# A three-block model on one core: shifts of the first norm on TensorE, its scales before the root, gates beside the query linear

## The reference

```python
cond_lat = silu(c); cond_ctx = silu(c_ctx)
m_lat = split(cond_lat @ mod_w[0] + mod_b[0], 6)      # shift, scale, gate, shift, scale, gate
m_ctx = split(cond_ctx @ mod_w[0] + mod_b[0], 6)
h_lat = rms_norm(x,   norm_g[0, 0]) * (1 + m_lat[1]) + m_lat[0]
h_ctx = rms_norm(ctx, norm_g[0, 0]) * (1 + m_ctx[1]) + m_ctx[0]
...                                                    # even_mixer: q, k, v = h @ w_in, ...
x = x + m_lat[2] * y_lat
```

## Time and profile before

| | us |
|---|---|
| three runs | 3272.82, 3277.46, 3280.25 |
| median | 3277.46 |
| the profiled execution's own time | 3262.18 |
| its span, first to last instruction | 3260.4 |
| TensorE busy | 2928.1 (90%) |
| DVE / ACT / GpSimd busy | 1280.6 / 989.3 / 991.1 |
| mean granted TensorE clock | 0.941 of 2.4 GHz |

### The profile page before, as it was taken

The page is one execution under the profiler, slowest core; times in us unless marked ns, Lnnn a source line. Parts: engine busy times, 40 slices in busy tenths (PEclk is TensorE's granted clock), DMA queues, the critical chain, the costliest instruction groups (busy, mean ns, idle before and its releaser), DMA issues. The chain is left out here.

```text
span 3260.4 us, 38562 instructions
## 1 busy us (share of the span) xinstructions
PE 2928.1 (90%) x15516; PEld 2363.9 (73%) x15516; DVE 1280.6 (39%) x1952; ACT 989.3 (30%) x1478; POOL 991.1 (30%) x478
## 2 busy tenths in 40 slices
PE   2889886679999999889998899999899999999998
PEld 1767775568888887868745777787678777886686
DVE  8466555571163125041016606511253454203523
ACT  2235554123211211422103323222244233325432
POOL 0220221113222222643102333444243443342343
PEclk7989898789999999999998999999899999999899
DMA  5300100321242113422103524332220111121121
GB/s 197 122 26 14 46 27 1 123 97 65 69 144 103 64 66 135 149 78 90 68 10 114 191 102 174 137 108 78 78 69 35 40 39 40 38 92 59 54 89 65
DMA packets 48963, 268.57 MB, mean 82 GB/s; under 512 B 5553, under 2 KB 6833, under 8 KB 28593
## 3 DMA queue, kind: packets, MB, share of 16 engines
q1 hardware_dynamic: 48816, 266.54, 23.5%
HBM read 264.42 MB, written 2.10 MB: 82 GB/s over the span
## 5 line engine op out<-in xcount | busy, mean ns | idle before, releaser
L422 POOL TENSOR_TENSOR shared_w_lo<-stage,shared_w_hi 128x2048 fp32r<-128x2048 f32 (+1 forms) x127 | 552.4, 4350 | 1338.6 <-ACT shared_w_hi L392 1336.0
L563 POOL TENSOR_TENSOR shared_w_lo<-stage,shared_w_hi 128x512 fp32r<-128x512 f32 (+2 forms) x233 | 297.6, 1306 | 625.8 <-ACT shared_w_hi L555 625.8
L392 ACT CAST shared_w_hi<-stage 128x2048 fp32r<-128x2048 f32 (+1 forms) x127 | 224.5, 1768 | 481.8 <-PE f0o_acc L485 135.7
L485 PE MATMUL f0i_acc<-norm_b_lo,shared_w_hi 128*128 128x512 f32 (+1 forms) x672 | 172.2, 338 | 0.0
L485 PE MATMUL f0i_acc<-norm_b_hi,shared_w_hi 128*128 128x512 f32 (+1 forms) x672 | 169.7, 333 | 2.0 <-PEq L369 2.0
L630 PE MATMUL two_acc<-norm_f_hi,shared_w_hi 128*128 128x512 f32 (+1 forms) x312 | 131.8, 422 | 9.1 <-DVE norm_f_lo L736 9.1
L828 DVE TENSOR_TENSOR ffn_hidden<-f0i_acc,ffn_gate 128x512 f32<-128x512 f32 (+1 forms) x44 | 22.5, 553 | 296.1 <-PE f0i_acc L485 288.5
L555 ACT CAST shared_w_hi<-stage 128x1024 fp32r<-128x1024 f32 (+2 forms) x117 | 114.7, 1022 | 70.4 <-PE last_acc L630 43.9
L485 PE MATMUL f1i_acc<-norm_e_hi,shared_w_hi 128*128 128x512 f32 x336 | 130.9, 390 | 2.2 <-PEq L369 1.5
L818 ACT CAST ffn_hi<-ffn_hidden 128x768 f32 (+3 forms) x44 | 32.0, 727 | 331.5 <-DVE ffn_hidden L828 331.5
L485 PE MATMUL f1i_acc<-norm_e_lo,shared_w_hi 128*128 128x512 f32 x336 | 130.7, 389 | 0.0
(11 more groups left out here) (577 smaller groups left out, 6955.3 us busy)
## 6 DMA issues: line engine op xcount, KB each, us to landing
stage<-in_w_f0i SPq DMA_DIRECT2D x22, 1024.0 KB, 4.9
stage<-in_w_f1i SPq DMA_DIRECT2D x22, 1024.0 KB, 4.9
stage<-in_w_rv SPq DMA_DIRECT2D x16, 1024.0 KB, 4.9
mod_slots_a<-in_w_mod SPq DMA_DIRECT2D x24, 512.0 KB, 4.8
stage<-in_w_rqk SPq DMA_DIRECT2D x12, 1024.0 KB, 4.9
mod_slots_f<-in_w_mod SPq DMA_DIRECT2D x24, 512.0 KB, 3.7
mod_slots_e<-in_w_mod SPq DMA_DIRECT2D x24, 512.0 KB, 5.5
stage<-in_w_dqkv SPq DMA_DIRECT2D x12, 1024.0 KB, 4.9
```

The costliest lines, as they stand in the source:

```text
L392: nc.scalar.copy(w_hi[:, slot, 0:size], stage[:, slot, 0:size]).then_inc(hi_ready, 1)
L422: nc.gpsimd.tensor_tensor(w_lo[:, slot, 0:size], stage[:, slot, 0:size], w_hi[:, slot, 0:size].bitcast(F32), ALU.subtract)\
L485: mm = nc.tensor.matmul(out[0:min(P, nt), b, 0:m], w[:, k, unit[1]:unit[1] + min(P, nt)], x[:, k, s:s + m], start=begin, stop=end)
L563: last = nc.gpsimd.tensor_tensor(w_lo[:, index % 2, part], stage[:, index % 2, part], w_hi[:, index % 2, part].bitcast(F32), ALU.subtract)
```

## The change

Three things are changed.

**Shifts on TensorE.** The 8 shift tiles leave `sum_up`. Their weights come in another layout (`w_shift`, two halves of two 1 MB loads), placed where `norm_a_hi` and `norm_a_lo` will be written later; the conditions come a second time, as 128 x 16 (`conds_turned`). TensorE sums a half in 8 matmuls of 2 x 512, ACT copies the 2 x 512 result out, TensorE turns it in four small transposes, and DVE adds the bias into `mods`. ACT's `norm_a_hi` of chunk c waits for its half. The copy of the second half stands in ACT's order before `norm_a_hi` of chunk 3; the bias add of half h stands in DVE's order behind `norm_squares` of chunk 4h.

**Scales ahead.** All 8 scale tiles (16 sums, as many as stood there before) and the 8 scale computations stand ahead of the reciprocal; the chunk loop holds no sums.

**Gates beside the query linear.** The 8 gate tiles are loaded and summed (16 sums) in the aq block, behind the norm; the akv block has none. The second aq weight tile is issued later, behind the second shift half. The unused product of a sum goes to SBUF instead of PSUM.

```diff
--- before.py
+++ after.py
@@ -662,11 +662,10 @@
             return [("F", c, segs) for c in range(0, nt, P)]
 
 
-        SCALES_AHEAD = 4
         norm_sem = {k: sem("norm_" + k) for k in ("squares", "summed", "root", "rstd", "scaled", "hi", "lo")}
         norms = [0]
 
-        def norm_split(x_of, groups, hi, lo, inputs=(), scales=None, home=None):
+        def norm_split(x_of, groups, hi, lo, inputs=(), scales=None, home=None, shifts=None, scales_ahead=0):
 
 
             n = norms[0]
@@ -704,7 +703,11 @@
                                                     scale=1.0 / D)
                     last.then_inc(S["root"], 1)
                     for c in range(DC):
+                        if shifts is not None:
+                            shifts["act"](act, c)
                         act.wait_ge(S["scaled"], done["scaled"] + c + 1)
+                        if shifts is not None:
+                            act.wait_ge(shifts["ready"], c // 4 + 1)
                         for s, m, _, b in groups:
                             last = nc.scalar.activation(hi[:, c, s:s + m], scaled[:, c % 2, s:s + m],
                                                         ACT.Identity, bias=b(c))
@@ -719,10 +722,12 @@
                             mm = nc.tensor.matmul(total[:, b, 0:m], ones[:], squares[:, c % 2, s:s + m],
                                                   start=c == 0, stop=c == DC - 1)
                         mm.then_inc(S["summed"], 1)
+                    if shifts is not None:
+                        shifts["pe"](pe)
 
                 def of_dve(dve):
                     if scales is not None:
-                        for c in range(SCALES_AHEAD):
+                        for c in range(scales_ahead):
                             scales(dve, c)
                         for landed_sem, count in inputs:
                             dve.wait_ge(landed_sem, count)
@@ -749,10 +754,12 @@
                                 scaled[:, c % 2, s:s + m], x_of(c, s, m), a(c), rstd[:, s:s + m],
                                 ALU.mult, ALU.mult)
                         last.then_inc(S["scaled"], 1)
+                        if shifts is not None:
+                            shifts["dve"](dve, c)
                         if c >= 1:
                             low(c - 1)
                         if scales is not None:
-                            scales(dve, c + SCALES_AHEAD)
+                            scales(dve, c + scales_ahead)
                     low(DC - 1)
 
                 return dict(act=of_act, pe=of_pe, dve=of_dve, ready=S["lo"], first=done["lo"])
@@ -1001,9 +1008,8 @@
 
             if c >= DC:
                 return
-            first_mod["sum_up"](dve, 2 * c)
-            first_mod["sum_up"](dve, 2 * c + 1)
-            dve.wait_ge(mod_summed, first_mod["sums_before"](2 * c + 2))
+            first_mod["sum_up"](dve, c)
+            dve.wait_ge(mod_summed, first_mod["sums_before"](c + 1))
             for v in range(2):
                 last = nc.vector.tensor_scalar(scale_of[:, 0, 0, v, c:c + 1], mods[:, 0, DC + c, v:v + 1], 1.0,
                                                mod_gain[:, 0, 0, c:c + 1], ALU.add, ALU.mult)
@@ -1094,9 +1100,52 @@
         first_scope = ExitStack()
         x_lat = sb(first_scope, "x_lat_in", [P, DC, LAT])
         x_ctx[0] = sb(first_scope, "x_ctx_in", [P, DC, CTX])
-        first_mod = modulation([(0, m, BOTH) for c in range(DC) for m in (c, DC + c)] + [(0, m, BOTH) for m in range(16, 24)],
+        first_mod = modulation([(0, m, BOTH) for m in range(DC, 3 * DC)],
                                sb(first_scope, "conds_a", [P, 2, D])[:], sb(first_scope, "mod_slots_a", [P, MOD_SLOTS, D]),
-                               psum(first_scope, "mod_product_a", [P, D])[:])
+                               sb(first_scope, "mod_product_a", [P, D])[:])
+        conds_t = sb(first_scope, "conds_turned", [P, DC, 2])
+        shift_row = sb(first_scope, "shift_row", [2, 2, 512])
+        w_shift = [[nc.alloc_sbuf_tensor_at(f"w_shift_{half}_{part}", [P, 4, 512], F32,
+                                            offset=places["norm_a_" + part] + half * 4 * TOK * 4)
+                    for part in ("hi", "lo")] for half in range(2)]
+        p_shift = psum(first_scope, "shift_sums", [P, 512])
+        p_shift_t = psum(first_scope, "shift_turned", [P, DC, 2])
+        sh = {k: sem("shift_" + k) for k in ("conds", "silu", "landed_0", "landed_1", "summed", "copied", "turned", "ready")}
+
+        def shift_pe(pe):
+
+            pe.wait_ge(sh["silu"], 1)
+            for half in range(2):
+                pe.wait_ge(sh[f"landed_{half}"], 32)
+                wait(pe, sh["copied"], half)
+                for k in range(DC):
+                    mm = nc.tensor.matmul(p_shift[0:2, :], conds_t[:, k, :], w_shift[half][k // 4][:, k % 4, :], start=k == 0,
+                                          stop=k == DC - 1)
+                mm.then_inc(sh["summed"], 1)
+                pe.wait_ge(sh["copied"], half + 1)
+                wait(pe, sh["ready"], half)
+                for j in range(4):
+                    mm = nc.tensor.transpose(p_shift_t[:, 4 * half + j, :], shift_row[:, half, j * P:(j + 1) * P], ident[0:2, 0:2])
+                mm.then_inc(sh["turned"], 1)
+
+        def shift_act(act, c):
+            if c in (0, 3):
+                half = c // 3
+                act.wait_ge(sh["summed"], half + 1)
+                nc.scalar.copy(shift_row[:, half, :], p_shift[0:2, :]).then_inc(sh["copied"], 1)
+
+        def shift_dve(dve, c):
+            if c % 4 == 0:
+                half = c // 4
+                dve.wait_ge(sh["turned"], half + 1)
+                bias = mod_bias[:, c:c + 4].rearrange("p (c o) -> p c o", o=1).broadcast_to([P, 4, 2])
+                nc.vector.tensor_tensor(mods[:, 0, c:c + 4, :], p_shift_t[:, c:c + 4, :], bias, ALU.add).then_inc(sh["ready"], 1)
+        def shift_load(sp, half):
+            for part in range(2):
+                sp.dma_start(w_shift[half][part][:], io["w_shift"][half][:, 4 * part:4 * part + 4, :])\
+                    .then_inc(sh[f"landed_{half}"], 16)
+
+        shifts_a = dict(pe=shift_pe, act=shift_act, dve=shift_dve, ready=sh["ready"])
 
         ctx_scope = ExitStack()
         ctx_loaded = sem("context_loaded")
@@ -1104,6 +1153,7 @@
             @block.sync
             def _(sp):
                 first_mod["load_conds"](sp)
+                sp.dma_start(conds_t[:], io["conds_t"]).then_inc(sh["conds"], 16)
                 first_mod["load"](sp, 0)
                 first_mod["load"](sp, 1)
                 sp.dma_start(ones[:], io["ones"]).then_inc(loaded, 16)
@@ -1111,28 +1161,36 @@
                 sp.dma_start(x_ctx[0][:], io["ctx"]).then_inc(ctx_loaded, 16)
                 for n in range(2, MOD_SLOTS):
                     first_mod["load"](sp, n)
-                issue_next(sp, 2)
+                shift_load(sp, 0)
+                issue_next(sp, 1)
 
             @block.scalar
             def _(act):
                 first_mod["silu_conds"](act)
+                act.wait_ge(sh["conds"], 16)
+                nc.scalar.activation(conds_t[:], conds_t[:], ACT.Silu).then_inc(sh["silu"], 1)
 
         def x_all(c, s, m):
             return x_lat[:, c, s:s + m] if s < LAT else x_ctx[0][:, c, s - LAT:s - LAT + m]
 
 
         norm_a = norm_split(x_all, [group(0, 0, 0, 0, LAT), group(0, 0, 1, LAT, CTX)], n_hi, n_lo,
-                            [(loaded, 48), (ctx_loaded, 16)], first_mods)
+                            [(loaded, 48), (ctx_loaded, 16)], first_mods, shifts=shifts_a, scales_ahead=DC)
 
         hn = {k: sem("headnorm_" + k) for k in ("tables", "squares", "summed", "root", "rstd", "normed", "rotated",
                                                "cosine", "sine", "done", "context")}
         window_ready = sem("window_loaded")
-        first_loads = dict(sp_first=lambda sp: [first_mod["load"](sp, n) for n in range(MOD_SLOTS, 2 * DC)], sp=lambda sp, t: None,
-                           act=lambda act, t: None, dve=lambda dve, t: None)
+        def first_issues(sp):
+            for n in range(MOD_SLOTS, DC):
+                first_mod["load"](sp, n)
+            shift_load(sp, 1)
+            issue_next(sp, 2)
+
+        first_loads = dict(sp_first=first_issues,
+                           sp=lambda sp, t: [first_mod["load"](sp, n) for n in range(DC, 2 * DC) if t == 0],
+                           act=lambda act, t: None,
+                           dve=lambda dve, t: [first_mod["sum_up"](dve, n) for n in range(DC, 2 * DC) if t == 0])
         linear("aq", n_hi, n_lo, feature_units(ALL), copy_units(qk, 0), source=norm_a, ahead=True, side=first_loads)
-        gate_mods = dict(sp=lambda sp, t: [first_mod["load"](sp, n) for n in range(2 * DC, 3 * DC)],
-                         act=lambda act, t: None, dve=lambda dve, t: [first_mod["sum_up"](dve, n) for n in range(2 * DC, 3 * DC)])
-
         def evac_akv(act, t, j, count, res):
```

(4 more changed lines are left out.)

## The result

| | before | changed |
|---|---|---|
| runs in the first comparison | 3267.79 to 3280.25, median 3272.82 (5) | 3234.46 to 3252.80, median 3238.36 (5) |
| ratio | | 0.9912, 95% interval 0.9891 to 0.9932 |
| profiled execution, span | 3260.4 us | 3251.2 us |
| mean granted clock of that execution | 0.941 | 0.944 |
| runs of the comparisons of this study, mean (e1's 12, below, make it 3269.6) | 3269.8 (89 runs) | 3240.6 (16 runs) |

The change makes the kernel faster by 29.2 us of 3269.8 (0.9%), with some 3.5 us of uncertainty from the scatter of the 16 runs; by the medians of the first comparison alone it would be 34.5. Two executions, of 6288 us (kernel before) and 9674 us (e14), are left out of all counts.

The account below looks back on a forecast made before the run. TensorE was taken to bound the whole span, DVE the start from 31 to 88 us. Gains of 21.1 up to the head stage and 1.0 in it make 22.1; 3277.46 - 22.1 = 3255.4, range 3250 to 3261, with rivals 3245 to 3266.

Parts of the forecast that it names:

- half 1 turned at 57.5: Shifts on TensorE during the norm: second half ready at 57.5 us, DVE asks at 59, so no cost on the path.
- two gate sums: Query linear's block: two gate sums collide with GpSimd instructions, 4.15 us charged for each, 8.3 in all.
- the clock down for the first 3.8 us of akv: Akv block's start: TensorE, having stood about 6 us, runs 3.8 us at 1.2 GHz; 1.9 us lost, bounds 0 and 2.5.
- Head at 127.35: Head stage's start: forecast at 127.35 us against 148.50 before, 21.1 us gained.
- The far bound for a product in SBUF: Sums' unused product in SBUF: at most 0.2 us more on each of 32 sums, 6.4 us; nothing was charged.
- gain 1.0 from starting at full clock: Head stage: it starts with TensorE at full clock, so 1.0 us gained, bounds 0 to 1.9.
- the base: Whole kernel: the start time 3277.46 us, median of the runs shown, from which 22.1 was taken.
- the part behind the head stage: From the head stage's start to the end: both kernels' spans were to differ by no more than 2 us.
- The gates were not free: Rival, query linear's block: collisions cost under 2.5 us, TensorE doesn't cool down; 30.0 us gained, 3247.5; chance 0.12.
- The shifts were not late: Rival, norm: late load of half 1 and fallen clock take 6.5 us of the gain, giving 3262; chance 0.14.
- A change that can't be told: Rival, whole kernel: 15.6 of the 22.1 us are lost, giving about 3271; chance 0.05.
- The clock afterwards: Rival, remaining 3110 us: TensorE's granted clock falls; a 1.2% fall loses 37 us, giving 3292; chance 0.04.

Follow-up runs that it names:

- e1: The kernel before, unchanged, run again as a control: 3268.1 us median of 12, ratio 0.9996.
- e14: The changed kernel with six extra VectorE instructions, each 8 elements wide, whose results nothing uses: mean 3235.1 ± 1.7 us.
- e4: The changed kernel with the last two gate tiles' four sums moved to the akv block: mean 3234.5 ± 3.5 us, ratio 0.9904.
- e5: The changed kernel with the second shift half summed three times on TensorE, a single execution: head stage's start at 129.6 us, rest 3116.3.
- e7: The kernel before with only the gates' loads and sums moved beside the query linear: 3270.6 us median of 10, ratio 1.0000.
- e2: The changed kernel, unchanged, run again: 3235.2 us median of 5, ratio 0.9904.
- e10: The changed kernel, unchanged, a third series on another chip: 3245.9 us median of 6, ratio 0.9925.
- e8: As e4, with the first shift half's load issued behind the sixth scale tile instead of ahead of the fifth: median 3236.1 us, ratio 0.9887.
- e11: The same kernel as e8, a later series: median 3227.7 us, ratio 0.9877.
- e12: The changed kernel with ten extra VectorE instructions in the akv block, each 8 elements wide: mean 3258.2 ± 1.7 us, ratio 0.9963.

## Why the prediction was wrong

**What held.** Reciprocal forecast at 44.8, measured 44.90; norm's end 68.2, measured 68.23; half 0 turned at 41.2, measured 39.8 (a matmul took 0.86 instead of 1.05; the 1.05 was not high for a lower clock, as I had written, since the earlier trace rows has 1.00 over 18.40 to 31.10); half 1 turned at 57.5, measured 56.9; VectorE asks for it at 59, measured 59.08 without a wait; two gate sums of 5.51 and 5.50, where 5.44 had been charged; VectorE last in the block at 99.4, measured 98.6; ScalarE's last copy 93.6, measured 93.98; the clock down for the first 3.8 us of akv, measured 0.59 over them. Head at 127.35, measured 126.15. The 1.2 us of surplus are 0.8 in the gates' sums (2.77 us from tile to tile with the product in SBUF, where I had taken 22.9 / 8 = 2.86) and 0.4 in the akv block (27.0 instead of 27.4; the clock cost 1.6, by e4, and the 2.8 of e5 and e7 lie outside of the bounds 0 and 2.5, so that the 1.9 was in part lucky). The far bound for a product in SBUF, 0.2 us a sum, is refuted: 1.28 as against 1.29.

**A small term that isn't fixed.** The head stage was to gain 1.0 from starting at full clock. Its first reciprocal before and in the changed kernel's first execution:

```profile
154.86 4.95 DVE L1330 RECIPROCAL head_rstd<-head_rstd 128x768 f32<-128x768 f32 x1 [6.08 <-ACT head_rstd L1280]
132.35 4.95 DVE L1388 RECIPROCAL head_rstd<-head_rstd 128x768 f32<-128x768 f32 x1 [5.92 <-ACT head_rstd L1338]
```

The clock was down there too in that execution (0.56 over 126.15 to 130.00), and from the head's start to this row it took 6.20 instead of 6.36: 0.16 gained. With the surplus above, the start as a whole gave 22.5, where 22.1 was forecast. It was down in e2 as well. In e10, the same program, it was 1.00 over 126.93 to 130.78, the way took 5.49 us, and the gain was 0.87. Nor is the other side fixed: in e1 the kernel before took 7.30. So the term can come out either way in one program.

**What failed is the sum's frame, in two terms of about 7 us.** First the base. "The median of the runs shown is 15.3 above the profiled execution, so I forecast 3277.46 - 22.1": the three runs shown were the 2nd, the 5th and the 25th highest of what came to be 89, whose mean is 3269.8. That is 7.7 of the 14.8 us between 3255.4 and 3240.6. Second, the part behind the head stage was held to be the same, to 2 us. By the timed runs it is some 7 us shorter on average, and the profiles show what that part does from one execution to the next: the granted clock falls, or doesn't, in three places of the delta rule's stage (e8 beside e11, 9 us) and in one stretch of some 100 us (e10 beside e4, 7 us). That no such scatter was allowed for is shown; why the changed kernel's mean comes out 7 us lower stays open, since its profiles have no shorter rest than those of the kernel before.

**The range** took 3.7 us from half the spread of three runs, and knew of no cost behind the head stage. One program's runs here spread over 20 us (changed) and 24 (before), and an edit that does no work can move the mean by 18 (e12). A forecast of 3269.8 - 22.1 = 3247.7, ± 8, would just have held 3240.6, and not the 3238.4 of the first comparison's median; base and width are chosen with hindsight. Nothing in three runs and one profile told me the base, but the spread of 7 us among three runs and the fourth execution 15 us under their median should have widened the range on that side.

**The rivals.** The gates were not free (the changed kernel's rows: two collisions, and TensorE waits 6.12 us; e4 gets 6.3 us back at the head). The shifts were not late, with 10.6 us of cover instead of 6 (e5). A change that can't be told is excluded by the ratio's interval, 0.9891 to 0.9932. The clock afterwards, named as the slower case, was the right place to look, since it moves the rest from one execution to the next; but the kernel did not become slower by it, and that it lowered the mean isn't shown. The collisions measured 4.2 each over the 1.28 of a free sum, beside the 4.15 charged. By the letter of the rule in the Trainium skill, "SBUF — State Buffer", section "Who interferes with whom", the prediction put them at up to 4.6; the trace agrees in kind, and each costs less than the whole, since the sums were issued 0.55 and 0.41 us behind GpSimd's start and ended 1.1 us behind its end.
